# Second attention: low keys laid on both halves of the rows, two buffers instead of three for the second map's exponentials

## The reference, cut to what matters

```
def diff_attend(q, k, v, lam):
    s = jnp.einsum('bqhmd,bkhmd->bhmqk', q, k, preferred_element_type=jnp.float32)
    a = jax.nn.softmax(s * (1.0 / math.sqrt(ATTN_HEAD_DIM)), axis=-1)
    a = a[:, :, 0] - lam * a[:, :, 1]
    return jnp.einsum('bhqk,bkhe->bqhe', a.astype(v.dtype), v)
```

## Time and profile before

| | us |
|---|---|
| median of three runs | 3266.9 |
| the profiled execution, its own time | 3265.95 |
| its span | 3264.5 |
| outside the span | 1.4 |
| TensorE busy in the span | 2961.1 (91%) |
| granted TensorE clock, mean of the span | 0.94 |

### The profile page before, as it was taken

How to read it: one execution, slowest core, us unless ns; L and a number is a source line. 1 busy time by engine, 2 the same in 40 slices (tenths; PEclk the granted TensorE clock), 3 DMA queues, 4 the chain that set the end, 5 groups by cost and what they waited for, 6 DMA issues and landing times.

```text
span 3264.5 us, 37958 instructions
## 1 busy us (share of the span) xinstructions
PE 2961.1 (91%) x15328; PEld 2449.8 (75%) x15328; DVE 1623.0 (50%) x1993; ACT 1267.3 (39%) x1943; POOL 260.3 (8%) x371
## 2 busy tenths in 40 slices
PE   7989899999999999999986899999989489999994
PEld 5778787788888988989876788756667267777773
DVE  3265565533343333333333532365653668888876
ACT  3233333231232122121223212166652268877774
POOL 1001110000000000000000000011121301111102
PEclk9988897999999999999998999979999789999997
DMA  4100000121213222222233211000030579999996
GB/s 156 39 20 7 14 20 20 34 58 46 97 47 91 66 78 83 60 89 61 74 96 103 72 35 52 13 1 1 1 121 36 193 249 365 365 359 361 366 366 208
DMA packets 283325, 368.98 MB, mean 113 GB/s; under 512 B 10748, under 2 KB 169904, under 8 KB 283152
## 3 DMA queue, kind: packets, MB, share of 16 engines
q1 hardware_dynamic: 269776, 322.08, 29.5%
q0 software_dynamic: 13376, 44.48, 4.3%
HBM read 341.26 MB, written 25.26 MB: 112 GB/s over the span
## 4 chain that ended last, share of the span: by engine, by line
PE 78%; issue 10%; DVE 5%; ACT 3%; DMA 2%; POOL 1%; SPq 0%; ACTq 0%; DVEq 0%; POOLq 0%
PE ps L414 75%; ACT r L389 1%; PE ps L1874 1%; POOL misc L819 1%; PE ps L2413 1%; PE ps L865 0%; ACT f L1939 0%; DVE r L398 0%; DMA f<-in_w_in_dram 0%; PE ps L2379 0%; PE ps L493 0%; DVE misc L1998 0%; DVE f L2274 0%; DVE f L2569 0%; DVE f L2517 0%
## 5 line engine op out<-in xcount | busy, mean ns | idle before, releaser
L414 PE MATMUL ps<-r,r 128*128 128x512 f32 (+3 forms) x11952 | 2461.9, 363 | 67.5 <-DVE r L398 46.3
L414 PEld LDWEIGHTS ps<-r,r 128*128 128x128 f32 (+1 forms) x11952 | 2018.3, 192 | 453.4 <-issue 98.9
L389 ACT ACTIVATE r<-f 128x2048 fp32r<-128x2048 f32 (+3 forms) x405 | 567.9, 1428 | 391.3 <-PE ps L414 373.3
L2337 DVE TENSOR_TENSOR r<-f,r 128x2048 fp32r<-128x2048 f32 x188 | 424.0, 2289 | 77.1 <-ACT r L389 77.1
L398 DVE TENSOR_TENSOR r<-f,r 128x1024 fp32r<-128x1024 f32 (+3 forms) x217 | 249.0, 1167 | 416.8 <-ACT r L389 416.5
L414 PE MATMUL ps<-f,f 128*128 128x128 f32 (+5 forms) x1442 | 285.6, 351 | 19.2 <-ACT f L920 14.8
L414 PEld LDWEIGHTS ps<-f,f 128*128 128x128 f32 (+2 forms) x1442 | 214.2, 222 | 57.8 <-issue 31.0
L1204 DVE TENSOR_TENSOR f<-ps,f 128x256 f32<-128x256 f32 x160 | 67.8, 424 | 242.7 <-PE ps L414 242.7
L672 DVE SCALAR_TENSOR_TENSOR f<-f,misc,f 128x1023 f32<-128x1023 f32 (+29 forms) x120 | 146.8, 1259 | 0.0
L1998 DVE TENSOR_REDUCE misc<-ps 128x1 f32<-128x1280 f32 x64 | 95.3, 1490 | 79.1 <-PE ps L414 79.0
L1377 ACT ACTIVATE r<-f 128x512 fp32r<-128x512 f32 x44 | 27.8, 632 | 210.8 <-DVE f L1403 210.8
(11 more groups left out here) (265 smaller groups left out, 1842.9 us busy)
## 6 DMA issues: line engine op xcount, KB each, us to landing
f<-in_w_gate_dram SPq DMA_DIRECT2D x64, 1024.0 KB, 13.5
f<-in_w_up_dram SPq DMA_DIRECT2D x64, 1024.0 KB, 10.7
f<-in_w_down_dram SPq DMA_DIRECT2D x64, 1024.0 KB, 10.5
f<-in_w_in_dram SPq DMA_DIRECT2D x68, 512.0 KB, 3.9
f<-in_w_ada_dram SPq DMA_DIRECT2D x48, 512.0 KB, 3.6
f<-in_w_ffn_in_dram SPq DMA_DIRECT2D x44, 512.0 KB, 4.7
f<-in_w_ffn_out_dram SPq DMA_DIRECT2D x24, 384.0 KB, 3.6
f<-in_w_out_dram SPq DMA_DIRECT2D x16, 512.0 KB, 4.3
```

The costliest lines, as they stand in the source:

```text
L389: self.act.activation(st.hi[st.slot[i]][:, 0:n], st.raw[i % len(st.raw)][:, 0:n], ACT.Copy).then_inc(self.sem(st.name + "_hi"), 1)
L414: return self.pe.matmul(o, left, right, start=start, stop=stop, skip_group_check=True)
L2337: self.dve.tensor_tensor(es.lo[i % 4], es.raw[i % 7], es.hi[i % 4].bitcast(F32), ALU.subtract).then_inc(self.sem("e_lo"), 1)
```

## The change

Low keys now lie on both halves of the rows, each map with a tile of its own, and the second matmul of a chunk runs over all 128 rows. It also adds the product low query·low key. VectorE makes the low keys on the rows that the high query takes ("own"), as before; GpSimd makes the same ones on the other 64 rows.

- The context's low keys (256 columns) get tiles of their own, "C". Low keys "L" of head parity 0 lie at 98 and 153 KB, those of parity 1 at 163 and 68 KB. 153 is a raw weight buffer of the convolution and 68 holds the queries of head 1.
- So head 0, map 1 gets its low keys inside the convolution, at its last tile (ct == 3), after all weight strips are split. VectorE waits there for its own low keys and for GpSimd's, since the last CV tile moves to 105, over head 0's keys. CV tile 3 is then the first to be split in the attention.
- In the odd heads, map 1, both engines wait for the low queries before they write the low keys to 68 KB.
- GpSimd: pool_conv2 for head 0; for the others pool_low_keys in its iterations 2 and 3, 7 and 8, 15 and 16 (whose squares ScalarE makes in its iterations 4 and 5, 9 and 10, 17 and 18), after the norm of that unit. Before its mod row it waits for sk_lp.
- PE waits for sk_lp too at the first unit of each head.
- PA: three buffers for map 0, two for map 1. exp of map 1 waits for the mix of u-2, exp of map 0 for the transposes as before.
- The raw buffers of the output weights move from 68, 72, 76, 109, 113 to 72, 76, 109, 113, 117; two rows of the shared semaphores are arranged anew.

```diff
-            L=self.r(o + 18, 1280)) for o in (80, 137)]
-        self.CV, self.u2 = [f(137 + 4 * ct, 1024) for ct in range(4)], f(165, 1024)
+        places = (dict(Q=(80, 84), K=(88, 93), L=(98, 153), C=(102, 157)),
+                  dict(Q=(137, 141), K=(145, 158), L=(163, 68), C=(167, 151.5)))
+        self.CV, self.u2 = [f(o, 1024) for o in (137, 141, 145, 105)], f(165, 1024)
-        self.PA = [[f(160 + 10 * j, 1280), f(165 + 10 * j, 1280)] for j in range(3)]
+        self.PA = [[f(168 + 5 * j, 1280) for j in range(3)], [f(183 + 5 * j, 1280) for j in range(2)]]
...
+    def pool_low_keys(self, h, mp):
+        other = (slice(64, 128), slice(0, 64))[mp]
+        if h % 2 and mp:
+            self.pool.wait_ge(*self.sem("sk_lo", 3 * (2 * h + mp) + 1))
+        for j, (k, high, low) in enumerate(self.low_keys(h, mp)):
+            self.pool.wait_ge(*self.sem("sk_hi", 5 * (2 * h + mp) + 2 + 2 * j))
+            self.pool.tensor_tensor(low[other, :], k, high.bitcast(F32), ALU.subtract).then_inc(self.sem("sk_lp"), 1)
+            self.pool.wait_ge(*self.sem("sk_lp", 2 * (2 * h + mp) + j + 1))
...
         self.dve_stack(0, 0)
-        self.dve_stack(0, 1)
+        self.dve_low_queries(0, 1)
         for ct in range(4):
             o = self.CV[ct]
             self.low(self.ws, self.i_cv + 3 * ct + 4)
+            if ct == 3:
+                dve.wait_ge(*sem("w_lo", len(self.ws.items)))
+                self.dve_low_keys(0, 1)
+                dve.wait_ge(*sem("sk_lo", 6))
+                dve.wait_ge(*sem("sk_lp", 4))
...
+    def pool_conv2(self):
+        self.pool_low_keys(0, 0)
+        self.pool.wait_ge(*self.sem("w_lo", len(self.ws.items)))
+        self.pool_low_keys(0, 1)
...
                 self.mm(o, q, sk["K"][mp][:, cs], True, False)
-                t = self.mm(o, q[r, :], sk["L"][r, cs], False, True)
+                t = self.mm(o, q, sk["L"][mp][:, cs] if c < 2 else sk["C"][mp], False, True)
...
-            if u >= 3:
+            if mp and u >= 2:
+                act.wait_ge(*sem("a2_mix", u - 1))
+            elif mp == 0 and u >= 3:
                 act.wait_ge(*sem("a2_pT", 3 * (u - 2)))
...
+            for h, at in ((1, 4), (2, NT + 1), (3, 2 * NT + 1)):
+                if u in (at - 2, at - 1):
+                    pool.wait_ge(*sem("a2_om", u + 1))
+                    self.pool_low_keys(h, u - at + 2)
```

More of the change, by code:

```diff
@@ L64 @@
      ("n4_hat", 8), ("xm_d", 8), ("aff", 5), ("tk", 33), ("ixf", 1), ("AB", 1), ("pick", 5), ("iT", 1), ("xst", 32)),
[L65 to L68, removed]
+    (("consts", 6), ("n1_inv", 2), ("zero", 1), ("qk_ones", 4), ("pj_inv", 32), ("a2_po", 64), ("n4_inv", 8),
+     ("e_lo_pool", 4), ("n5_inv", 8)),
+    (("pj_aug", 32), ("n2_inv", 2), ("xc_inv", 2), ("n3_inv", 2), ("sk_lp", 16)),
+    (("a2_om", 32), ("anti", 2), ("o2_inv", 8), ("out_pool", 2)),
 )
@@ L1718, in act_stack, with low_keys, dve_low_queries @@
             act.activation(sk["K"][mp][other, c], k, ACT.Copy).then_inc(sem("sk_hi"), 1)
-    def dve_stack(self, h, mp):
-        dve, sem = self.dve, self.sem
+    def low_keys(self, h, mp):
+        own = (slice(0, 64), slice(64, 128))[mp]
+        sk = self.stacks[h % 2]
+        return ((self.K2[own, h, :], sk["K"][mp][own, 0:1024], sk["L"][mp]),
+                (self.K2c[own, h, :], sk["K"][mp][own, 1024:1280], sk["C"][mp]))
+    def dve_low_queries(self, h, mp):
         own, other = ((slice(0, 64), slice(64, 128)), (slice(64, 128), slice(0, 64)))[mp]
@@ L1724, in dve_stack @@
         sk, n = self.stacks[h % 2], 5 * (2 * h + mp)
[L1725 to L1731, removed]
+        self.dve.wait_ge(*self.sem("sk_hi", n + 1))
@@ new lines, in dve_low_queries, with dve_low_keys @@
+        self.dve.tensor_tensor(sk["Q"][mp][other, :], self.Q2[own, h, :], sk["Q"][mp][own, :].bitcast(F32),
+                               ALU.subtract).then_inc(self.sem("sk_lo"), 1)
+    def dve_low_keys(self, h, mp):
+        own = (slice(0, 64), slice(64, 128))[mp]
+        if h % 2 and mp:
+            self.dve.wait_ge(*self.sem("sk_lo", 3 * (2 * h + mp) + 1))
+        for j, (k, high, low) in enumerate(self.low_keys(h, mp)):
+            self.dve.wait_ge(*self.sem("sk_hi", 5 * (2 * h + mp) + 2 + 2 * j))
+            self.dve.tensor_tensor(low[own, :], k, high.bitcast(F32), ALU.subtract).then_inc(self.sem("sk_lo"), 1)
@@ L1735, in pe_conv2, with dve_stack @@
+    def dve_stack(self, h, mp):
+        self.dve_low_queries(h, mp)
+        self.dve_low_keys(h, mp)
     def pe_conv2(self):
@@ L1852, in scores @@
             h, i = self.PAIRS[u]
-            sk, r = self.stacks[h % 2], slice(64 * mp, 64 * mp + 64)
+            sk = self.stacks[h % 2]
             if u:
@@ L1858, in scores @@
                 pe.wait_ge(*sem("sk_lo", 3 * (2 * h + 2)))
+                pe.wait_ge(*sem("sk_lp", 2 * (2 * h + 2)))
             q = sk["Q"][mp][:, i * P:(i + 1) * P]
@@ L1938, in copy_p @@
                     act.wait_ge(*sem("a2_pv", u - 1))
+                elif u == 1:
+                    act.wait_ge(*sem("mc_lo", 1))
                 act.copy(o.rearrange("p a b -> p (a b)"), ps[:, 6 + k % 2, 0:(4, 4, 2)[g] * P]).then_inc(
@@ L1980, in act_attention2 @@
                     act.wait_ge(*sem("cv2_mm", 24))
[L1981 removed]
+                ct = (u + 3) % 4
+                act.activation(self.MX[0][:, 4 + ct, :], self.CV[ct], ACT.Copy).then_inc(sem("mc_hi"), 1)
             for h, at in ((1, 4), (2, NT + 1), (3, 2 * NT + 1)):
@@ L2014, in mix @@
             dve.wait_ge(*sem("a2_fac", 3 * u + 3))
-            dve.scalar_tensor_tensor(out=self.PA[j][0], in0=self.PA[j][1], scalar=r_[1], in1=self.PA[j][0],
+            dve.scalar_tensor_tensor(out=self.PA[0][j], in0=self.PA[1][u % 2], scalar=r_[1], in1=self.PA[0][j],
                                      op0=ALU.mult, op1=ALU.add).then_inc(sem("a2_mix"), 1)
@@ L2062, in pool_attention2 @@
                 pool.wait_ge(*sem("sk_hi", 40))
+                pool.wait_ge(*sem("sk_lp", 16))
                 self.pool_mod_row("g1", self.G1, self.g1_tmp, 2, "norm_post_mix_2")
@@ L2665, in pool_program @@
         self.pool_lambda()
+        self.pool_conv2()
         self.pool_attention2()
```

14 lines of the change are left out of this document (8 added, 6 removed).

## The result

The changed kernel takes 3220.7 us (median of four runs, 3216.14 to 3223.71) against 3269.18 for the kernel before on the same chip: ratio 0.985, 95% interval 0.9833 to 0.9867. Forecast were 3210 with a range of 3195 to 3235.

What follows compares the result with a forecast made beforehand. TensorE, busy 91% of the span, was taken as the bound, over half a steady unit's time going to score matmuls. Savings of 39 + 15 + 4 - 2 = 56 us off 3265.95 gave 3210 us, range 3195 to 3235.

Steps and rivals of the forecast that it cites:

- the two engines at once: VectorE and GpSimd making low keys together could stretch some pieces; bounds 0 and 6 x 1 us, 2 taken in all.
- steady units (18): Second attention's steady stretches: 18 units from 8.47 to 6.3 us save 39 us, bounds 26 and 42.
- stretches around the stacks (3): Three slower units around each head's stacks: 4.95 us saved a stretch, 15 for three, bounds 9 and 20.
- opening: Second attention up to its fourth unit: shorter score tiles save 4 us, bounds 0 and 10.
- added work: New low-key pieces and waits at head 0 and in the attention: 2 us lost in all.
- Score matmuls: With all six matmuls over 128 rows a score tile takes 1.16 us against 2.32, twice a unit; saving bounds 0 and 1.16.
- Steady unit: Unit after the change: TensorE alone 6.15 us, loop through VectorE and ScalarE 6.2; 6.3 taken, bounds 6.15 and 7.0.
- saving of 1.39 us per stack unit: Units with stacks: map 1's scores, behind TensorE's wait, go from 3.71 to 2.32 us at the lower clock.
- Added work at head 0: Low keys at the last convolution tile fit VectorE's 13.94 us idle gap: cost 0; without that cover 3 to 5 us, once.
- The clock did not fall in steady stretches: Rival: clock stays at 1.2 GHz in steady stretches, a unit costs 11.4 us; 3310 us, chance 0.04.
- ScalarE and VectorE did not become the bound of a steady unit: Rival: more latency in these engines makes a unit 7 us or over; 3232 us, up to 3240, chance 0.14.
- The loads did not stay in turn: Rival: score tiles' weight loads still alternate with matmuls; 3266 us or some us more, chance 0.03.

Runs made afterwards that it cites:

- e3: The changed kernel, with GpSimd starting its low keys of a stack only when VectorE has finished its own of that stack; 3210.86 us, ratio 0.9817.
- e1: The kernel before, with the second matmul of a chunk over all 128 rows of the tile holding both maps' low keys; 3212.08 us, ratio 0.9815.
- e2: The changed kernel, with the second matmul of a chunk again over the 64 rows of the high query; 3266.21 us, ratio 0.9996.
- e4: The kernel before, with a score tile's three matmuls over 128 rows first, then the three over 64; 3225.7 us, ratio 0.9874.
- e12: The changed kernel itself once more, on the same chip as e13; 3219.16 us, ratio 0.9852.
- e13: The kernel of e3 once more, beside e12 on the same chip; 3207.75 us, ratio 0.9823.
- e10: Against e3, stack copies of heads 2 and 3 spread over seven iterations, on ScalarE ahead of exp of map 1; 3194.82 us, ratio 0.9774.
- e9: Against e3, stack copies spread over six iterations a head at the iteration's end, g1 row operations one an iteration; 3227.48 us, ratio 0.9864.

## Why the prediction was right, point by point

It was right in its direction, its mechanism and its range; the forecast was 11 us too low, and most of that is one term that was mis-sized, the two engines at once. The terms against what the traces of after and e3 show, in us saved from before, counted between the same reductions of map 1 (the opening after is 35.07 us, before 38.2):

| term | forecast | after | e3 |
|---|---|---|---|
| steady units (18) | 39 | 152.5 - 120.6 = 32.0 | 152.5 - 115.8 = 36.7 |
| stretches around the stacks (3) | 15 | 106.3 - 95.9 = 10.4 | 106.3 - 89.6 = 16.7 |
| opening | 4 | 3.1 | 3.1 |
| added work | -2 | in the rows above | in the rows above |
| sum | 56 | 45.5 | 56.5 |

That e3 comes out at the forecast is in part chance: its steady units save less than forecast and its stretches more. The whole spans differ from before by 44.9 and 52.4 us, since what lies around the attention scatters.

**Score matmuls: right, a little optimistic.** Priced at 1.16 us a tile, measured 1.25. The step "what differs is that every second matmul covers 64 rows" is shown by e1 and e2, and e4 makes it exact: it is the change between heights. The weight loads to the same rows do hide, so the rule on row groups in the Trainium skill ("TensorE: Matmul & The Clock Gate", Part 3, What overlaps and what doesn't), by which the change would have gained nothing, fails here a second time: 0.205 us a load (1.23 / 6), one behind the other. The Trainium skill ("TensorEngine Tiling (Array Packing)", Key Properties) says that a change of tiling mode drains TensorE. e4 agrees, if 64 and 128 rows are two modes: the idle time stands at the changes of height and nowhere else.

**Steady unit: right, with some luck.** Forecast 6.3; a unit takes 6.3 to 6.4 (2345.94 to 2352.23 and on to 2358.62 between the reductions of map 1). The loop through VectorE and ScalarE is not what binds: with the tile at its measured 1.25 us TensorE, its wait of 0.24 us included, needs 8.47 - 2 x 1.07 = 6.33. The forecast came to the same by two errors that cancel, tiles 0.09 us too short and 0.15 us for waits that don't come. What is missing of the 39 us is not in such units. The first unit behind each stretch takes 7.7 to 8.15 us (6.29 in e3, so that loss belongs to the term below), and one unit near the end 8.68, as long as before. There VectorE makes the g1 row in three operations, 3.7 us, that slower scores used to cover; I had not named that cover. These rows show its first and last operation:

```profile
2360.28 1.22 DVE L2130 TENSOR_TENSOR f<-f,f 128x1024 f32<-128x1024 f32 x1
...
2362.78 1.22 DVE L2134 TENSOR_TENSOR f<-f,f 128x1024 f32<-128x1024 f32 x1
...
2363.93 1.48 DVE L2042 TENSOR_REDUCE misc<-ps 128x1 f32<-128x1280 f32 x1
```

**The term that was mis-sized: "That both engines work at once could stretch some: ... bounds 0 and 6 x 1 us; I take 2 in all".** It costs 10 to 11 us, above the upper bound too (after against e3: 9.8 us in the medians, 11.4 in e12 and e13, 251.58 against 240.46 between the first and the last reduction of map 1). Nothing is shared out between the two engines; by the rows one waits for the other's whole instruction. VectorE's 256 columns take 0.42 us alone and 2.55 beside GpSimd's 1024: in the first iteration of head 3 they end at 2277.84, 0.27 us behind GpSimd's piece. GpSimd's 1024 take 2.98 us after and 2.36 in e3, and in e3, the other way round, its 256 take 1.86 beside the mix. The Trainium skill ("SBUF — State Buffer", SBUF: two separate sides) says that the two engines hold a port pair by an exclusive lock for a whole instruction when VectorE has two SBUF inputs and GpSimd reads SBUF; I did not weigh it. The trace agrees, also in that the reduction, with its one input in PSUM, is not slowed. The step that failed is the reason for the low end, "since ScalarE and TensorE set these units"; once TensorE is fast, VectorE's delay is on the path. e2 shows that before that point it isn't. And the saving of 1.39 us per stack unit did not come as one: the two stack units of after take 12.9 and 13.3 us, longer than the 12.1 to 12.5 and 13.1 to 13.2 of before, and all of the stretch's gain is in the third, 5.79 us in place of 9.5 to 10.35. In e3 the two take 11.3 and 11.4 to 11.6: 1.3 to 1.45 us saved in each, so the price of 1.39 was right for a stack without the two engines at once.

**Added work at head 0: right.** VectorE still stood idle 10.31 us (13.94 in the earlier trace rows) before the convolution's next product:

```profile
2087.65 3.76 DVE L1744 TENSOR_TENSOR r<-f,r 64x1024 fp32r<-64x1024 f32 x2
2101.72 0.69 DVE L1810 TENSOR_TENSOR f<-ps,f 128x512 f32<-128x512 f32 x1 [10.31 <-PE ps L416]
```

**Rivals.** The clock did not fall in steady stretches (PEclk 1.00 in all three). ScalarE and VectorE did not become the bound of a steady unit. The loads did not stay in turn.

**The tile's missing 0.09 us** is not in the matmuls of 256 columns. These take 0.12 us each, as in the earlier trace rows: in the tile of 2350.29 they start at 2351.30 and 2351.42, and the transpose behind them at 2351.54. The four of 512 columns before them take 1.01 us where 0.91 was priced, and 0.09 of it lies at the first of them, which stands 0.32 us ahead of the second. Why the first is slower stays open.

## What to carry to other kernels

Matmuls over 64 and over 128 rows side by side should be grouped by height, or brought to one height: order alone gave 43 of the 48 us here, and e1's single line, whose extra product is not of the reference, more than the whole change. Work that is handed to GpSimd so that it runs beside VectorE's two-input operations on SBUF can cost more than it relieves; give it a start that falls beside reductions from PSUM. Idle time of an engine is not one pool: a piece of 1.04 us was free in one place of ScalarE's order and cost over 1 us in another, so look which wait the place stands ahead of.

## What the runs showed of the hardware that I had not expected

- A change of matmul height costs 0.14 to 0.18 us each way, seen as 0.25 us of "issue" idle of the weight loads; loads and matmuls of 64 rows are otherwise as fast as those of 128.
- VectorE's 64x256 subtraction: 0.42 us alone, 2.55 us beside a GpSimd subtraction of 1024 columns; its mix of 1280 columns: 1.55 us alone, 3.67 beside the same (e10). The reduction from PSUM takes 1.48 us either way.
- The granted clock fell also behind waits well under the 2.53 us of the earlier trace rows: in e9 TensorE waited 0.84, 0.73 and 1.19 us within 3.24 us, the granted clock then went from 1.00 to 0.63, and the values after it took 3.21 us.
